# Attention, output projection and feed-forward of an encoder step: three phases against one merged phase

## The chip, the cores and the metric

The kernel runs on one core of one Trainium2 chip. The metric is device time in microseconds (us): the median of three runs before the change is 3194.27 us (3193.53 to 3196.78). The core has five engines with a queue of instructions each: TensorE (PE in the profile, its weight loads PEld), VectorE (DVE), ScalarE (ACT), GpSimd (POOL) and SyncE (SP, which here only issues DMAs). An engine takes its instructions in the order written, and a semaphore makes it wait for another engine.

## The reference

One layer over 2048 prompt rows and 64 sample rows (T = 2112) of width 1024. What the change touches comes after the input projection and the gated linear attention:

```python
def sb_block(q, q_pos, k, v):                       # stick-breaking attention, 4 heads x 64
    z = jnp.einsum('bqhd,bkhd->bhqk', q, k).astype(jnp.float32) * (SB_DH ** -0.5)
    mask = k_pos[None, :] < q_pos[:, None]
    lk = jnp.where(mask, jax.nn.log_sigmoid(-z), 0.0)
    ...                                             # after = sum of lk over the later keys
    A = jnp.exp(jnp.where(mask, jax.nn.log_sigmoid(z) + after, -jnp.inf))
    return jnp.einsum('bhqk,bkhd->bqhd', A.astype(v.dtype), v)
...
out = jnp.concatenate([go, so, co], axis=-1) @ w_out
x = layer_norm(DEEPNORM_ALPHA * x + mix, ln1_g[l], ln1_b[l])
ff = jnp.square(jax.nn.relu(x @ w_up[l])) @ w_down[l]          # 1024 -> 4096 -> 1024
x = layer_norm(DEEPNORM_ALPHA * x + ff, ln2_g[l], ln2_b[l])
```

The exponential of a sum of log-sigmoids is a product of sigmoids, so the kernel computes sigmoid(z) times the running product of sigmoid(-z) over the later keys.

## The kernel before, in words

Five phases run one after the other, with a barrier of all engines between them: `phase_in` (layer norm, x @ w_in), `phase_gla`, `phase_sb` (line 995), `phase_out` (line 1374) and `phase_ffn` (line 1552). The first two are not changed.

**Products in parts.** A float32 operand is split into a high half (rounded to fp32r, by a ScalarE copy) and a low half (operand minus high half, a VectorE subtraction). `split_product` (line 109, its three matmuls are lines 111 to 113) adds high x high, high x low and low x high.

**phase_sb.** Rows are taken in groups of 512 queries; for each head and each block of 512 keys there are four *slots*, one for each 128 queries (168 slots in all, 96 of them over 512 unmasked keys, 64 on the diagonal, 8 of the sample rows). A slot is: scores on TensorE (`ps_z`, three matmuls), two sigmoids on ScalarE (`tg` line 1229, `sg` line 1230), the running product on VectorE (`keep`, the scan of line 1272), and its product with `sg` (`aw`), on VectorE (line 1279) or for every second slot on GpSimd (line 1303). Six slots later `aw` is transposed by TensorE (line 1365, `ps_a`), copied as high half by ScalarE (`ath`, line 1239) and subtracted by VectorE (`atl`, line 1286), and two slots after that multiplied with the values (`ps_o`, three matmuls). Scores and transposes have three PSUM banks each. Queries, keys and values of all rows are kept in SBUF.

**phase_out.** The mixed columns (`mixt_scratch`) times `w_out`, whose halves stay in SBUF; then the residual and layer norm 1 tile by tile (128 rows); its result goes to `x1_scratch` in DRAM.

**phase_ffn.** Groups of 512, 512, 512 and 576 rows. For each group both weight matrices pass through SBUF in units of 128 x 2048 (1 MB): loaded by SP, high half by ScalarE (`wh`, line 1721), low half by VectorE (`wl`, line 1769), in a ring of three. A step `up` makes two blocks of 128 hidden columns (`ps_u`, 24 matmuls for each block and each part of the rows), ScalarE takes relu (line 1738), VectorE squares (line 1783), ScalarE copies the high half (`hh`, line 1743), VectorE subtracts (`hl`, line 1786). A step `down` multiplies eight hidden blocks with `w_down` (`ps_d`) and VectorE adds the result to `res` (line 1761). Between groups TensorE transposes the next rows (line 1842, one bank `ps_t`). Layer norm 2 is VectorE's, with an addition on GpSimd (line 1824).

The order of the work is a list made by Python before any instruction is written (`plan` in `phase_sb`, `order` in the other two); every engine goes through the same list and issues its own part of each entry.

## Time and profile before

| | |
|---|---|
| median of three runs | 3194.27 us |
| span of the profiled execution | 3213.5 us |
| TensorE busy in it | 2880.8 us (90%) |
| VectorE / ScalarE / GpSimd busy | 1621.9 / 1042.7 / 405.2 us |
| mean granted TensorE clock | 0.929 |

The page gives no other time for the profiled execution than its span, which is 19.2 us above the median. Busy is the time in which an engine had an instruction under way; ends of TensorE's matmuls are modelled, and neighbours overlap, so the distance between the starts of two matmuls tells what one costs, and not its duration. The granted clock is a share of full speed: 1.0 is 2.4 GHz, 0.5 is 1.2 GHz. In these times `phase_sb` runs from about 955 us, `phase_out` from about 1395 us and `phase_ffn` from about 1596 us of the span to its end.

### The profile page before, as it was taken

What the parts mean: (1) busy time and instruction counts of PE and PEld (TensorE: products, weight loads), DVE (VectorE), ACT (ScalarE), POOL (GpSimd) and SP (SyncE); (2) the same over time, 40 slices, a digit from 0 to 9 for tenths busy, and PEclk for the clock granted to TensorE, in tenths of its full rate; (3) what the DMA queues carried; (4) which work ended last, traced back from release to release, by engine and by line L of the source; (5) the groups of instructions that cost most, each with busy time, mean ns of one, the idle gap of its engine ahead of it and who ended that gap; (6) DMA issues with size and microseconds to landing.
All of it is one profiled execution on the core that took longest, in us unless ns stands there. A gap on an engine that the chain in (4) does not pass through costs nothing.

```text
span 3213.5 us, 35264 instructions
## 1 busy us (share of the span) xinstructions
PE 2880.8 (90%) x13930; PEld 2308.0 (72%) x13930; DVE 1621.9 (50%) x2127; ACT 1042.7 (32%) x1670; POOL 405.2 (13%) x316
## 2 busy tenths in 40 slices
PE   5999999945559999889879998999989998999998
PEld 4778788834446555567668886888778886889986
DVE  5333331178867999847443343634345433534434
ACT  3333332224435666631032222323222222213321
POOL 1100100076301222203200000200001000100001
PEclk9999999957785899979979998999989998999999
DMA  5445453233322000034243322333223332222221
GB/s 187 162 152 170 162 162 111 85 118 94 78 68 64 23 6 4 11 133 173 85 145 105 118 93 78 118 107 116 92 73 125 122 104 66 79 92 79 79 79 43
DMA packets 206421, 318.23 MB, mean 99 GB/s; under 512 B 17296, under 2 KB 116416, under 8 KB 206256
## 3 DMA queue, kind: packets, MB, share of 16 engines
q1 hardware_dynamic: 177264, 255.26, 25.3%
q0 software_dynamic: 10160, 34.62, 2.9%
q10 hardware_dynamic: 18832, 26.10, 2.2%
q8 instruction: 111, 1.82, 0.2%
q14 instruction: 54, 0.44, 0.0%
HBM read 254.96 MB, written 60.96 MB: 98 GB/s over the span
## 4 chain that ended last, share of the span: by engine, by line
PE 47%; DVE 2%; ACT 1%; issue 0%; DMA 0%; POOL 0%; SPq 0%; ACTq 0%; POOLq 0%
PE p_ps_d L111 8%; PE p_ps_d L112 8%; PE p_ps_d L113 8%; PE p_ps_u L111 7%; PE p_ps_u L112 7%; PE p_ps_u L113 7%; PE p_ps_t L1842 1%; DVE p_xl L1774 1%; ACT p_xh L1728 1%; DVE p_wl L1769 0%; DVE p_res L1814 0%; DVE p_r L1783 0%; ACT p_hh L1743 0%; DVE p_res L1811 0%; ACT p_r L1738 0%
## 5 line engine op out<-in xcount | busy, mean ns | idle before, releaser
L1769 DVE TENSOR_TENSOR p_wl<-p_wst,p_wh 128x2048 fp32r<-128x2048 f32 x128 | 293.3, 2292 | 375.1 <-ACT p_wh L1721 375.1
L111 PE MATMUL p_ps_u<-p_xh,p_wh 128*128 128x512 f32 (+1 forms) x1280 | 453.9, 355 | 14.1 <-DVE p_r L1783 9.2
L113 PE MATMUL p_ps_u<-p_xl,p_wh 128*128 128x512 f32 (+1 forms) x1280 | 453.4, 354 | 0.0
L112 PE MATMUL p_ps_u<-p_xh,p_wl 128*128 128x512 f32 (+1 forms) x1280 | 453.3, 354 | 0.0
L111 PE MATMUL p_ps_d<-p_wh,p_hh 128*128 128x512 f32 (+1 forms) x1088 | 430.3, 395 | 10.4 <-DVE p_hl L1786 10.4
L112 PE MATMUL p_ps_d<-p_wh,p_hl 128*128 128x512 f32 (+1 forms) x1088 | 428.0, 393 | 0.0
L113 PE MATMUL p_ps_d<-p_wl,p_hh 128*128 128x512 f32 (+1 forms) x1088 | 426.9, 392 | 0.0
L1721 ACT ACTIVATE p_wh<-p_wst 128x2048 fp32r<-128x2048 f32 x128 | 244.1, 1908 | 555.7 <-PE p_ps_d L113 549.3
L111 PEld LDWEIGHTS p_ps_u<-p_xh,p_wh 128*128 128x128 f32 x1280 | 243.6, 190 | 45.8 <-DVE p_r L1783 10.1
L113 PEld LDWEIGHTS p_ps_u<-p_xl,p_wh 128*128 128x128 f32 x1280 | 243.5, 190 | 30.2
L112 PEld LDWEIGHTS p_ps_u<-p_xh,p_wl 128*128 128x128 f32 x1280 | 243.5, 190 | 29.9
L1824 POOL TENSOR_TENSOR p_res<-p_res,p_b_b 128x1024 f32<-128x1024 f32 (+1 forms) x17 | 64.1, 3773 | 1527.8 <-DVE p_res L1814 1527.8
L111 PEld LDWEIGHTS p_ps_d<-p_wh,p_hh 128*128 128x128 f32 (+1 forms) x1088 | 203.6, 187 | 59.0 <-DVE p_hl L1786 11.9
L111 PE MATMUL p_ps_m<-p_xh,p_wh 128*128 128x512 f32 (+3 forms) x680 | 242.3, 356 | 1.4 <-DVE p_xl L320 1.4
L112 PE MATMUL p_ps_m<-p_xh,p_wl 128*128 128x512 f32 (+3 forms) x680 | 243.0, 357 | 0.0
L113 PE MATMUL p_ps_m<-p_xl,p_wh 128*128 128x512 f32 (+3 forms) x680 | 241.3, 355 | 0.0
L329 DVE TENSOR_TENSOR p_wl<-p_wst,p_wh 128x512 fp32r<-128x512 f32 (+1 forms) x192 | 127.3, 703 | 223.6 <-ACT p_wh L272 223.5
L113 PEld LDWEIGHTS p_ps_d<-p_wl,p_hh 128*128 128x128 f32 (+1 forms) x1088 | 203.2, 187 | 48.1
L112 PEld LDWEIGHTS p_ps_d<-p_wh,p_hl 128*128 128x128 f32 (+1 forms) x1088 | 203.8, 187 | 46.0
L1783 DVE SCALAR_TENSOR_TENSOR p_r<-p_ps_u,p_r 128x512 f32<-128x512 f32 (+1 forms) x160 | 95.4, 596 | 213.9 <-ACT p_r L1738 213.9
L1761 DVE SCALAR_TENSOR_TENSOR p_res<-p_res,p_ps_d 128x512 f32<-128x512 f32 (+1 forms) x136 | 93.5, 687 | 173.0 <-PE p_ps_d L113 162.2
L1738 ACT ACTIVATE p_r<-p_ps_u 128x512 f32<-128x512 f32 (+1 forms) x160 | 83.4, 521 | 290.9 <-PE p_ps_u L113 290.8
(173 smaller groups left out, 4788.9 us busy)
## 6 DMA issues: line engine op xcount, KB each, us to landing
p_wst<-in_w_up SPq DMA_DIRECT2D x64, 1024.0 KB, 5.4
p_wst<-in_w_down SPq DMA_DIRECT2D x64, 1024.0 KB, 5.0
p_wst<-in_w_in SPq DMA_DIRECT2D x128, 256.0 KB, 3.7
zt_scratch<-p_outb ACTq DMA_DIRECT2D x48, 256.0 KB, 2.0
p_wst<-in_w_in SPq DMA_DIRECT2D x32, 264.0 KB, 3.2
p_xs<-in_x_prompt SPq DMA_DIRECT2D x16, 512.0 KB, 5.5
xn_scratch<-p_xn POOLq DMA_DIRECT2D x16, 512.0 KB, 3.1
p_wst<-in_w_in SPq DMA_DIRECT2D x64, 128.0 KB, 2.6
```

What stands on the lines that cost most here:

```text
L111: pe.matmul(out, lhs_hi, rhs_hi, start=first, stop=False, skip_group_check=skip)
L112: pe.matmul(out, lhs_lo, rhs_hi, start=False, stop=False, skip_group_check=skip)
L113: return pe.matmul(out, lhs_hi, rhs_lo, start=False, stop=last, skip_group_check=skip)
L329: dve.tensor_tensor(wl[:, gc % 2, k, :width], wst[:, u % WSTAGE, :width], wh[:, gc % 2, k, :width].bitcast(F32), ALU.subtract).then_inc(wl ...
L1721: act.activation(wh[:, u % WRING, :], wst[:, u % WSTG, :], ACT.Copy).then_inc(whi_done, 1)
L1728: act.activation(xh[:, 4 * q:4 * q + 4, o:o + c], ps_t[:, :].rearrange("p (k t) -> p k t", k=4)[:, :, :c], ACT.Copy).then_inc(xhi_done, 1)
L1738: act.activation(r[:, i % 2, :cc], ps_u[:, i % 2, :cc], ACT.Relu).then_inc(relu_done, 1)
L1761: dve.scalar_tensor_tensor(out=acc, in0=acc, scalar=ALPHA if c == 0 else 1.0, in1=ps_d[:cc, ti, :], op0=ALU.mult, op1=ALU.add).then_inc(su ...
L1769: dve.tensor_tensor(wl[:, u % WRING, :], wst[:, u % WSTG, :], wh[:, u % WRING, :].bitcast(F32), ALU.subtract).then_inc(wlo_done, 1)
L1774: dve.tensor_tensor(xl[:, 4 * q:4 * q + 4, o:o + c], ps_t[:, :].rearrange("p (k t) -> p k t", k=4)[:, :, :c], xh[:, 4 * q:4 * q + 4, o:o + ...
L1783: dve.scalar_tensor_tensor(out=r[:, i % 2, :cc], in0=ps_u[:, i % 2, :cc], scalar=0.0, in1=r[:, i % 2, :cc], op0=ALU.max, op1=ALU.mult).the ...
L1824: pool.tensor_tensor(res[:c, g % 2, ti, :], res[:c, g % 2, ti, :], b_b[:c, :], ALU.add).then_inc(normed, 1)
```

## The change

`phase_sb`, `phase_out` and `phase_ffn` become one function, `phase_tail` (line 989 of the kernel after), with one list `order`.

- **Two streams.** The stream `dense` holds the output projection and feed-forward of the four groups of rows, the stream `attention` the slots. Group 0's attention and the preparation of all keys and values come first. From there on, `add_attention` puts pieces of the attention stream behind dense steps in proportion to a price of each step (5.4 for `up`, 2.7 for `down` and `out`), such that attention of group g is complete before the output projection of group g. The stretch from the last quarter of an output projection to the transposes behind it has price 0 and gets none, and so does the whole feed-forward of the last group. A `pause` of price 32.4 behind the first output projection puts some attention there without products beside it.
- **Attention in two passes.** Keys are stored in DRAM with their high half in partitions 0 to 63 and the low half in 64 to 127 (`ks_scratch`), the query's halves are present in both; one matmul with 128 rows does both products with the key (lines 1758 and 1759). Values lie as high | low in 128 columns (`vs_scratch`), so each output has two halves of 64 partitions that are added at the end (line 1652). A head takes 256 queries at a time, so the products with the values are twice as many, of up to 256 columns, in two passes (lines 1784 and 1785). Keys, values and queries are loaded anew for each head and block.
- **Banks.** `ps_z`, `ps_a` and `ps_o` have one PSUM bank each, `ps_d` three, `ps_u` two. The transposes between groups use `ps_d`.
- **Weights.** Units of 128 x 1024 (512 KB), 288 in all, ring of four, two stages. The low half is subtracted on GpSimd (line 1669) and not on VectorE. `w_out` passes through the same ring once for each group.
- **Feed-forward.** Chunks of four hidden blocks and not eight, so VectorE adds 272 results of `down` and 68 of `out` (136 and 34 before). ScalarE makes the high half as the square of relu (line 1479); VectorE squares the SBUF copy (line 1592).
- **Layer norm.** Two VectorE instructions of 1024 columns (lines 1556 and 1559) take the place of two on VectorE and one on GpSimd; the root of the variance is a power on GpSimd, 128 x 1 (line 1665), and not a square root on ScalarE. Layer norm 1 stays in SBUF (`x1_scratch` is gone).

```diff
-def phase_sb(nc, a, zt_dram, mixt_dram, k_p, v_p, k_s, v_s):
-    ZB, AB = 3, 3
-    SIG, AW, AT = 4, 3, 3
-    TURN_LAG, WEIGH_LAG = 6, 8
...
-def phase_out(nc, mixt_dram, w_out, ln_g, ln_b, xn_dram, x1_dram):
-    RAW, STAGE, BANKS = 4, 4, 6
...
-def phase_ffn(nc, x1_dram, w_up, w_down, ln_g, ln_b, ident_in, y_tile, lasting):
-    NF = 8
-    WRING, WSTG = 3, 2
+def phase_tail(nc, a, zt_dram, mixt_dram, xn_dram, ks_dram, vs_dram, k_p, v_p, k_s, v_s, y_tile, lasting):
+    NF = 4
+    WRING, WSTG, DB = 4, 2, 3
+    SIG, KEEP, AW = 2, 3, 3
...
+        ps_u, ps_d = s.ps("ps_u", [P, 2, 512]), s.ps("ps_d", [P, DB, 512])
+        ps_z, ps_a, ps_o = s.ps("ps_z", [P, 512]), s.ps("ps_a", [P, 512]), s.ps("ps_o", [P, 512])
...
+        for g in range(SEQ // 512):
+            for b in range(2):
+                for h in range(SBH):
+                    diag = (g, 512, [(0, P), (P, P)], [P * (2 * b + 1), P * (2 * b + 2)], [(P * x, P, max(0, x - 2 * b)) for x in range(2 * b + 2)])
+                    full = [(c, 512, [(0, P), (P, P)], [512, 512], [(P * x, P, 0) for x in range(4)]) for c in range(g - 1, -1, -1)]
+                    add_head(h, 512 * g + 256 * b, 256, [diag] + full)
...
+        due, at = [], 0.0
+        for u, _, _ in items:
+            at = max(units[u]["slot1"] + 1, at + 0.5)
+            due.append(int(at))
...
+        cost = {"up": 5.4, "down": 2.7, "out": 2.7, "pause": 2.7}
+        price = [0.0 if i in quiet or i >= mixed[-1] else cost.get(st[0], 0.0) * (st[1] if st[0] == "pause" else 1) for i, st in enumerate(dense)]
...
+        def add_attention(upto):
+            nonlocal put
+            order.extend(attention[put:upto])
+            put = max(put, upto)
...
+        def split_weights(i):
+            nonlocal next_w
+            while next_w < len(wunits) and (next_w < WRING or unit_end[next_w - WRING] < i):
+                order.append(("w", next_w))
+                if next_w + WSTG < len(wunits):
+                    order.append(("w_load", next_w + WSTG))
+                next_w += 1
...
+        begun, spent = put, 0.0
+        for i, st in enumerate(dense):
+            if i in mixed:
+                add_attention(group_end[st[1]])
+            if st[0] in ("up", "down", "out"):
+                order.append(st)
+                split_weights(i)
+            elif st[0] == "mix":
+                order.append(st)
+                if st[2] + 4 < KT:
+                    order.append(("mix_load", st[1], st[2] + 4))
+            elif st[0] != "pause":
+                order.append(st)
+            spent += price[i]
+            if i < mixed[-1]:
+                add_attention(begun + int((len(attention) - begun) * spent / sum(price)))
+        assert put == len(attention) and next_w == len(wunits)
...
-                            act.activation(hh[:, slot_of(c, f), o:o + cc], r[:, i % 2, :cc], ACT.Copy).then_inc(sq_done, 1)
+                        act.activation(hh[:, hidden_at(c, f), o:o + cc], r[:, i % 2, :cc], ACT.Square).then_inc(hh_done, 1)
...
-                    dve.tensor_tensor(wl[:, u % WRING, :], wst[:, u % WSTG, :], wh[:, u % WRING, :].bitcast(F32), ALU.subtract).then_inc(wlo_done, 1)
-                            dve.scalar_tensor_tensor(out=r[:, i % 2, :cc], in0=ps_u[:, i % 2, :cc], scalar=0.0, in1=r[:, i % 2, :cc],
+                        dve.tensor_tensor(r[:, i % 2, :cc], r[:, i % 2, :cc], r[:, i % 2, :cc], ALU.mult).then_inc(sq_done, 1)
...
-                    dve.tensor_scalar(acc, acc, mv[:c, sl, 0:1], rstd[:c, sl, :], ALU.subtract, ALU.mult).then_inc(centred, 1)
-                    dve.tensor_tensor(acc, acc, g_b[:c, :], ALU.mult).then_inc(scaled, 1)
-                    pool.tensor_tensor(res[:c, g % 2, ti, :], res[:c, g % 2, ti, :], b_b[:c, :], ALU.add).then_inc(normed, 1)
+                dve.scalar_tensor_tensor(out=acc, in0=acc, scalar=mv[:c, 0:1], in1=g_b[:c, :], op0=ALU.subtract, op1=ALU.mult).then_inc(scaled, 1)
+                dve.scalar_tensor_tensor(out=acc, in0=acc, scalar=rstd[:c, :], in1=b_b[:c, :], op0=ALU.mult, op1=ALU.add).then_inc(ln_done, 1)
...
+                    pool.tensor_tensor(rstd[:c, :], veps[:c, :], power[:c, :], ALU.pow).then_inc(rstd_done, 1)
+                if what == "w":
+                    u = at[0]
+                    pool.wait_ge(whi_done, u + 1)
+                    pool.tensor_tensor(wl[:, u % WRING, :], wst[:, u % WSTG, :], wh[:, u % WRING, :].bitcast(F32), ALU.subtract).then_inc(wlo_done, 1)
...
-                        mm = split_product(pe, out, qh[pb:pb + 64, pr, q], ql[pb:pb + 64, pr, q], kh[pb:pb + 64, pr, ks_], kl[pb:pb + 64, pr, ks_],
+                        pe.wait_ge(sig_done, 2 * n)
+                    pe.matmul(ps_z[:m, :w], qh[:, sl, o:o + m], kk[:, u % 2, :w], start=not un["diag"], stop=False, skip_group_check=True)
+                    pe.matmul(ps_z[:m, :w], ql[:, sl, o:o + m], kk[:, u % 2, :w], start=False, stop=True, skip_group_check=True).then_inc(z_done, 1)
...
-            mm = split_product(pe, ps_o[:, u["o"] % 2, c0:c1], vh[:kn, vt, hc], vl[:kn, vt, hc], ath[:kn, ai % AT, c0:c1], atl[:kn, ai % AT, c0:c1],
+                    for x, (k0, kn, i0, off, nq) in enumerate(turned_columns(k)[0]):
+                        out, vs = ps_o[:, P * i0:P * i0 + nq], vv[:kn, u % 2, y + x, :]
+                        pe.matmul(out, vs, ath[:kn, k % 2, off:off + nq], start=opens and x == 0, stop=False, skip_group_check=True)
+                        mm = pe.matmul(out, vs, atl[:kn, k % 2, off:off + nq], start=False, stop=k + 1 == heads[j]["item1"], skip_group_check=True)
+                    mm.then_inc(av_done, 1)
...
-        phase_sb(nc, a, zt_dram, mixt_dram, k_p, v_p, k_s, v_s)
-        phase_out(nc, mixt_dram, a["w_out"][0], a["ln1_g"][0], a["ln1_b"][0], xn_dram, x1_dram)
-        phase_ffn(nc, x1_dram, a["w_up"][0], a["w_down"][0], a["ln2_g"][0], a["ln2_b"][0], a["ident"], y_tile, lasting)
+        phase_tail(nc, a, zt_dram, mixt_dram, xn_dram, ks_dram, vs_dram, k_p, v_p, k_s, v_s, y_tile, lasting)```

**ScalarE's queue in the feed-forward.** `p_r` is relu, `p_hh` the high half of the hidden block, `p_wh` that of a weight unit. Before, in the first group:

```order
L1721 ACTIVATE p_wh<-p_wst 128x2048 x5
L1738 ACTIVATE p_r<-p_ps_u 128x512
L1743 ACTIVATE p_hh<-p_r 128x512
L1738 ACTIVATE p_r<-p_ps_u 128x512
L1743 ACTIVATE p_hh<-p_r 128x512
L1721 ACTIVATE p_wh<-p_wst 128x2048
```

Now, in the first group as well (`p_tg`, `p_sg` are the sigmoids of a slot, `p_ath` the high half of transposed weights of attention, `p_otmp` a head's output):

```order
L1472 ACTIVATE p_r<-p_ps_u 128x512
L1479 ACTIVATE p_hh<-p_r 128x512
L1449 ACTIVATE p_wh<-p_wst 128x1024
L1524 ACTIVATE p_otmp<-p_ps_o 64x256
L1509 ACTIVATE p_tg<-p_ps_z 128x512
L1510 ACTIVATE p_sg<-p_ps_z 128x512
L1517 ACTIVATE p_ath<-p_ps_a 128x384
L1449 ACTIVATE p_wh<-p_wst 128x1024
```

The sigmoids and the copy for attention stand behind relu, square and weight copy of the dense step that they follow.

**VectorE's queue in the feed-forward.** `p_wl` is the low half of a weight unit, `p_hl` that of the hidden block, `p_res` the sum. Before:

```order
L1783 SCALAR_TENSOR_TENSOR p_r<-p_ps_u,p_r 128x512
L1786 TENSOR_TENSOR p_hl<-p_r,p_hh 128x512
L1769 TENSOR_TENSOR p_wl<-p_wst,p_wh 128x2048 x2
L1761 SCALAR_TENSOR_TENSOR p_res<-p_res,p_ps_d 128x512 x4
L1769 TENSOR_TENSOR p_wl<-p_wst,p_wh 128x2048 x2
```

Now (`p_keep` is the scan, `p_aw` its product with `sg`, `p_atl` the low half of the transposed weights, `p_ql` that of a query):

```order
L1640 TENSOR_TENSOR p_aw<-p_sg,p_keep 128x512
L1540 SCALAR_TENSOR_TENSOR p_res<-p_res,p_ps_d 128x512
L1630 SCALAR_TENSOR_TENSOR p_keep<-p_tg,p_keep,p_zero 128x513
L1540 SCALAR_TENSOR_TENSOR p_res<-p_res,p_ps_d 128x512
L1645 TENSOR_TENSOR p_atl<-p_ps_a,p_ath 128x512
L1615 TENSOR_TENSOR p_ql<-p_qraw,p_qh 128x256
L1540 SCALAR_TENSOR_TENSOR p_res<-p_res,p_ps_d 128x512
L1645 TENSOR_TENSOR p_atl<-p_ps_a,p_ath 128x512
L1540 SCALAR_TENSOR_TENSOR p_res<-p_res,p_ps_d 128x512 x2
```

The weight halves are gone from this queue, and single additions alternate with pieces of a slot.

**GpSimd's queue.** Before, at the end of attention and the start of the output projection:

```order
L1303 TENSOR_TENSOR p_aw<-p_sg,p_keep 128x256
L1303 TENSOR_TENSOR p_aw<-p_sg,p_keep 128x512 x7
L1303 TENSOR_TENSOR p_aw<-p_sg,p_keep 64x512 x4
L74 UNCONDITIONAL_BRANCH
L76 ISA
L1507 UNCONDITIONAL_BRANCH
L1515 TENSOR_TENSOR p_y<-p_y,p_b_b 128x1024
```

Now, across the change from one group of rows to the next:

```order
L1669 TENSOR_TENSOR p_wl<-p_wst,p_wh 128x1024 x4
L1678 TENSOR_TENSOR p_aw<-p_sg,p_keep 128x512
L1669 TENSOR_TENSOR p_wl<-p_wst,p_wh 128x1024 x2
L1665 TENSOR_TENSOR p_rstd<-p_veps,p_power 128x1 x3
L1669 TENSOR_TENSOR p_wl<-p_wst,p_wh 128x1024 x2
L1665 TENSOR_TENSOR p_rstd<-p_veps,p_power 128x1
L1669 TENSOR_TENSOR p_wl<-p_wst,p_wh 128x1024 x5
```

GpSimd has the weight halves, every second slot's product and the power of each layer norm in one queue.

## Rows read from the trace of the kernel before

**Rows 1.** Stages: busy us (count) of PE, PEld, DVE, ACT, POOL; clock; DMA share; GB/s
```profile
955.00:1395.00 440.00, 391.40 (x1718) 241.00 (x1718) 373.44 (x497) 262.27 (x601) 91.82 (x84) 0.82 0.09 24
1399.00:1596.00 197.00, 190.28 (x816) 153.88 (x816) 117.41 (x172) 31.14 (x55) 48.31 (x32) 0.97 0.42 148
1596.00:1634.70 38.70, 8.82 (x32) 5.73 (x32) 10.20 (x15) 8.67 (x11) 2.88 (x2) 0.53 0.35 117
1634.70:1966.40 331.70, 328.86 (x1441) 271.96 (x1442) 132.70 (x122) 95.10 (x94) 0.00 (x0) 0.99 0.34 111
1966.40:1984.10 17.70, 7.54 (x34) 5.15 (x32) 5.95 (x9) 4.18 (x7) 0.00 (x0) 0.61 0.00 0
3198.00:3213.50 15.50, 2.51 (x11) 1.21 (x9) 6.26 (x9) 0.29 (x1) 5.79 (x4) 0.64 0.25 85
```

**Rows 2.** PE in time order in the feed-forward: start, duration, line, tiles
```profile
1700.13 0.39 PE L111 MATMUL p_ps_d<-p_wh,p_hh 128*128 128x512 f32 x1
...
1705.80 0.39 PE L112 MATMUL p_ps_d<-p_wh,p_hl 128*128 128x512 f32 x1
...
2899.76 0.29 PE L113 MATMUL p_ps_u<-p_xl,p_wh 128*128 128x288 f32 x1
...
2904.67 0.29 PE L111 MATMUL p_ps_u<-p_xh,p_wh 128*128 128x288 f32 x1
```

**Rows 3.** PE in time order: one slot of the attention stage
```profile
1248.34 0.49 PE L111 MATMUL p_ps_z<-p_kh,p_qh 64*128 64x512 f32 x1
...
1249.23 0.66 PE L1365 MATMUL p_ps_a<-p_ident,p_aw 128*128 128x128 f32 x4
1249.64 0.47 PE L111 MATMUL p_ps_o<-p_ath,p_vh 128*64 128x512 f32 x1
...
1250.49 0.49 PE L111 MATMUL p_ps_z<-p_kh,p_qh 64*128 64x512 f32 x1
```

**Rows 4.** Groups of the attention stage: busy, mean ns of one | idle before
```profile
L1272 DVE TENSOR_TENSOR_SCAN p_keep<-p_tg,p_keep,p_zero 128x512 f32<-128x512 f32 x96 | 149.6, 1558 | 11.6 <-ACT p_tg L1229 11.6
L1286 DVE TENSOR_TENSOR p_atl<-p_ps_a,p_ath 128x512 fp32r<-128x512 f32 x112 | 75.7, 678 | 3.8 <-ACT p_ath L1239 3.8
L1239 ACT ACTIVATE p_ath<-p_ps_a 128x512 fp32r<-128x512 f32 x112 | 67.6, 603 | 10.5 <-PE p_ps_a L1365 10.0
L1230 ACT ACTIVATE p_sg<-p_ps_z 128x512 f32<-128x512 f32 x112 | 66.4, 593 | 0.0
```

**Rows 5.** Groups of the output projection and the feed-forward
```profile
L1452 ACT ACTIVATE p_wh<-p_wst 128x1024 fp32r<-128x1024 f32 x8 | 8.5, 1060 | 10.6 <-DMA p_wst<-in_w_out 10.6
L1505 DVE TENSOR_TENSOR p_y<-p_y,p_g_b 128x1024 f32<-128x1024 f32 x16 | 19.6, 1227 | 0.5
L1515 POOL TENSOR_TENSOR p_y<-p_y,p_b_b 128x1024 f32<-128x1024 f32 x16 | 39.3, 2457 | 153.7 <-DVE p_y L1505 153.7
L1743 ACT ACTIVATE p_hh<-p_r 128x512 fp32r<-128x512 f32 x96 | 60.8, 633 | 96.0 <-DVE p_r L1783 96.0
L1761 DVE SCALAR_TENSOR_TENSOR p_res<-p_res,p_ps_d 128x512 f32<-128x512 f32 x128 | 88.1, 688 | 171.7 <-PE p_ps_d L113 161.7 <-DVE p_res L1761 0.5
L1802 DVE BATCH_NORM_STATS2 p_stats<-p_res 128x6 f32<-128x512 f32 x16 | 11.0, 689 | 0.1
```

**Rows 6.** VectorE and GpSimd side by side in layer norm 2
```profile
2025.29 2.29 DVE L1769 TENSOR_TENSOR p_wl<-p_wst,p_wh 128x2048 fp32r<-128x2048 f32 x1
2025.52 4.33 POOL L1824 TENSOR_TENSOR p_res<-p_res,p_b_b 128x1024 f32<-128x1024 f32 x1 [423.56 <-DVE p_res L1814]
...
2028.87 1.53 DVE L1786 TENSOR_TENSOR p_hl<-p_r,p_hh 128x512 fp32r<-128x512 f32 x1 [0.70 <-ACT p_hh L1743]
...
2031.70 0.69 DVE L1786 TENSOR_TENSOR p_hl<-p_r,p_hh 128x512 fp32r<-128x512 f32 x1 [0.70 <-ACT p_hh L1743]
```

**Rows 7.** DMA issues of the page: KB each, us to landing
```profile
p_wst<-in_w_up SPq DMA_DIRECT2D x64, 1024.0 KB, 5.4
```

**Rows 8.** Small GpSimd operation of the convolution, by form
```profile
L959 POOL COPY p_cu<-p_cu 128x2 f32<-128x2 f32 x6 | 4.5, 742 | 21.1 <-DMA p_cb<-zt_scratch 21.1
```

1420 lines of the change are left out of this document (659 added, 761 removed).

## The prediction, made before the changed kernel ran

> **What bounds the kernel now.** I read the stages first [rows 1]: from 955 us to the end, 2258.5 us, the work is in the three phases that the change merges. In the steady feed-forward TensorE is the bound: 328.9 us of 331.7 busy at a granted clock of 0.99, with VectorE at 132.7 us. The time order there [rows 2] shows an even beat: 25 matmuls of 512 columns from 1700.13 to 1705.80, so 0.227 us each, and 37 of 288 columns from 2899.76 to 2904.67, so 0.133 us each. The attention stage is different: 440 us in which VectorE is busy for 373 and TensorE for 391. One of its slots [rows 3] takes 2.15 us: scores 0.89, four transposes 0.41, products with values 0.85. VectorE needs almost the same for a slot [rows 4]: scan 1.56, subtraction 0.68, half a product of 0.69 (the size of rows 6), 2.6 us with the waits in it. So there neither leaves much to the other, but the stage also starts badly: mean clock 0.82, where the feed-forward has 0.99. Between the stages TensorE nearly stands: 38.7 us with 8.8 busy before the feed-forward, 17.7 with 7.5 at a change of group, each at a clock of 0.53 to 0.61.
>
> **Dense products.** The change leaves their number alone: 2304 matmuls of 512 columns for `up` in groups 0 to 2, 1536 of 288 in group 3, 3264 for `down`, 816 for the output projection. 6384 x 0.2268 = 1448 us, 1536 x 0.1327 = 204, and 34 times four transposes at 0.41 [rows 3] = 14. Sum 1666 us.
>
> **TensorE's part of attention.** One score matmul of three goes (0.89 - 0.23 = 0.66 us), the transposes stay (0.41), and instead of three products of 512 columns a slot has four of up to 256. No row has 256 columns; below stands 0.113 us (half of 0.227), above 0.133 (the row with 288). I take 0.13, so 0.53 plus 0.09 for the switch. A full slot is 1.69 us, for 2.15. 96 x 1.69 = 162; 64 diagonal slots with shorter operands at 1.3, my estimate from the same parts, = 83; 8 sample slots and 42 transposes of keys 12. Sum 257 us, of which some 25 (19 slots) lie in the opening, before any dense product, and 232 among or between dense steps. The gain is that VectorE's 2.6 us per slot now stand beside dense products, and the stretches at low clock go: TensorE is what the time is made of.
>
> **The opening.** It prepares all keys and values, six blocks, one staging buffer each, and runs 19 slots. A block: twice (transposes 0.41, two copies at 0.60, two subtractions at 0.68) = 5.9 us, a copy of 1.06 and a subtraction of 1.23 [rows 5] for the values, then stores that must land before the next block writes, about 3: 11 us. Three slots of group 0 between, at some 3 us each, since with one bank for scores the next slot waits for both sigmoids. 6 x 20 = 120 us. Bounds: 75 if the slots fit into the waits of the blocks, 150 if they don't and each DMA costs the 5.4 us of the largest one [rows 7].
>
> **The first group and the borders.** The first products wait for mixed rows, 8 us. Behind the first output projection the pause has four slots and two layer norms that nothing covers, then eight groups of transposes: 24 us beyond the slots counted above. At each of three group changes the output projection must wait until relu, square and low half of the last `up` and four split inputs are through: 0.6 + 0.6 + 4 x 0.87 and a few waits, 6 us; and the first `up` waits for the last transposes, 5 us; with some us at the lower clock behind each, as after the stops in rows 1, 15 us for a change that now costs 17.7. 45 us. Layer norm 1 stands between four `out` steps of 2.7 us: two statistics of 0.69, two instructions of 1.23 [rows 5] and the power on GpSimd, for which VectorE waits. The power has no row: it is at most the 0.74 us of a small copy [rows 8], at least nothing, but a weight half of 2.46 us can stand before it. 5 to 6 us for each of four tiles against 13.6 us of products and two spare banks leaves about 4 us, over four groups 15. The end (last addition, layer norm, store) is 15.5 us now and 14 without GpSimd's addition.
>
> **Weight halves on GpSimd.** 288 units at 2.46 us [rows 5] are 708 us of a queue with almost nothing else, beside some 2000 us. A unit's way behind an `up`: relu 0.6, square 0.63, high half 1.06, low half 2.46: 4.75 us, and the ring lets it be needed only after another step of 24 x 0.227 = 5.44 us. The load is half the bytes of the 5.4 us DMA [rows 7], and with two stages a stage has two steps for load, high and low half: 5.4 + 1.06 + 2.46 = 8.9 against 10.9. So I cost this at nothing, covered by dense products. If the cover goes (low half at 4.33, [rows 6]) the two figures are 10.85 against 10.9: just even. VectorE loses 128 x 2.29 = 293 us of halves [rows 6] and gains 170 additions x 0.69 = 117 [rows 5]; it was no bound in the feed-forward and needs about 60% of the time there with attention.
>
> **New waits.** The list gives every engine one order, with one bank each for scores and for transposes. The second block of transposes of a unit waits for VectorE's low half of the first, behind the scan, behind the sigmoids, which stand in ScalarE's queue behind relu, square and weight copy of the step in front. From the end of an `up`: 0.6 + 0.63 + 1.06 + 0.6 = 2.9 us to the first sigmoid's end, at which GpSimd has just begun a low half; scan 1.56 (a mean with some waits in it; up to 2.4 more behind a low half), low half 0.68, and some tenths for signals: between 5.5 and 8 us. Cover: scores 0.66, transposes 0.41 and one `up`, 6.5; with a `down` in its place 3.8. In the new list the two blocks of transposes follow each other with no dense step between only 8 times in 156, transposes and their products with values 5 times. So a wait per slot lies between 0 and, where a `down` is the only cover, 2 to 3 us; most pairs have an `up` or two `down`s. I take 0.4 us for each of 149 slots: 60 us.
>
> **Sum.** 955 (unchanged) + 120 + 8 + 24 + 1666 + 232 + 45 + 15 + 14 = 3079 us without new waits, 3139 with them. The profiled execution before has a span of 3213.5 us, the median is 3194.3, so a factor of 0.994: **3120 us**, 74 us (2.3%) less.
>
> **GpSimd and VectorE on one pair of ports.** A low half of 2.29 us on VectorE and an addition begun 0.23 us later on GpSimd took 4.33 us, and VectorE's next subtraction of two SBUF operands took 1.53 us where one alone took 0.69 [rows 6]: they ran one after the other. With attention, for each group, GpSimd's 72 x 2.46 = 177 us and VectorE's scans, squares, subtractions, products and norms of two SBUF operands (50 x 1.56 + 64 x 0.69 + 25 x 0.69 + 16 x 1.23 = 159 us) take turns: 336 of some 460 us. That fits, with queueing that the 0.4 us above hold. The Trainium skill (SBUF — State Buffer, section "SBUF: two separate sides") says that the pair is locked for a whole instruction and the loser is blocked fully; by that rule the case is the third rival below, the trace agrees with the rule, and it does not show which engine wins when both queue up.
>
> **Rivals.**
> 1. *The waits are covered fully* and the opening overlaps well (75 us). For it: the 13 adjacent pairs are few. Against: in the attention stage of now one signal chain already limits. 3079 - 45 = 3034, x 0.994 = 3016 us.
> 2. *The chain through one bank is the bound* (slower). Every unit waits at TensorE for a low half, as if covered by a `down` alone. At 1.6 us for each of 149 slots 238 us, 3317 in the profile, 3297 us. It decides from 0.9 us per slot on (3213.5 - 3079 = 134.5 over 149). For it: lag of two slots instead of six, one bank instead of three. Against: dense steps between nearly all pairs.
> 3. *The shared ports make weight halves late.* Low halves at 4.33 us, the stage loop at its limit, 1 us more for each of 96 `up` units beside attention: 3139 + 96 = 3235, 3216 us.
> 4. *The change does not hide anything*: TensorE's work in attention was 391 of 440 us. Had it all to be paid again, 955 + 120 + 1666 + 391 + 106 = 3238, 3218 us. Against it: the busy time overlaps and is at a low clock; the starts of rows 3 give 257.
>
> **How the numbers follow.** Forecast (3065 to 3180 us) 0.62; rival 1 0.15; rival 2 0.12; rivals 3 and 4 together 0.08; 0.03 within 0.2% of 3194 us, which is about what a measurement of this kernel can tell from no change. Faster: 0.62 + 0.15 and 0.01 of the third's lower side = 0.78; same 0.03; slower 0.19. The range reaches into rival 1 and over rivals 3 and 4: 3015 to 3225 us. It leaves out rival 2 and part of rival 1.
>
> **What would show it.** Right: TensorE beats of 0.227 us with attention in between at a clock near 1; the low-half line of GpSimd at 2.3 to 2.6 us mean, and few waits of TensorE for it; a first dense product at about 1083 us; an end of group 0's feed-forward some 450 us after its first `up`. Wrong: transposes of attention waiting for the low half line 1645 by more than 60 us in sum, and the clock at 0.5 in short pieces through the groups (rival 2); a mean of 4 us on line 1669 and waits of the first matmul of an `up` for it (rival 3); TensorE's starts in a slot no closer than 2.15 us (rival 4); an opening of over 150 us.

## The result: 4.6% slower, not 2.3% faster

| | before | after |
|---|---|---|
| median (lowest to highest), us | 3193.90 (3193.49 to 3196.78) | 3342.76 (3335.89 to 3348.53) |
| span of the profiled execution, us | 3213.5 | 3334.1 |
| mean granted TensorE clock | 0.929 | 0.917 |

The ratio is 1.0459, with a 95% interval of 1.0442 to 1.0475. The forecast of 3120 us and its range of 3015 to 3225 are both missed, on the far side of no change.

The page of the changed kernel: busy time and share of each engine, three groups of instructions (busy us, mean ns | idle time of the engine before them and what ended it), the granted clock in 40 slices, and one DMA.

```profile
PE 2791.5 (84%) x13838; PEld 2299.2 (69%) x13838; DVE 1672.1 (50%) x2175; ACT 1077.0 (32%) x1783; POOL 1072.1 (32%) x571
...
PEclk9999999868865889999998999989899998999998
...
L1669 POOL TENSOR_TENSOR p_wl<-p_wst,p_wh 128x1024 fp32r<-128x1024 f32 x288 | 742.9, 2594 | 1098.5 <-ACT p_wh L1449 1098.5
L1540 DVE SCALAR_TENSOR_TENSOR p_res<-p_res,p_ps_d 128x512 f32<-128x512 f32 (+1 forms) x340 | 231.9, 684 | 491.0 <-PE p_ps_d L113 470.3
...
L1771 PE MATMUL p_ps_a<-p_ident,p_aw 128*128 128x128 f32 (+2 forms) x564 | 101.7, 305 | 173.8 <-DVE p_atl L1645 143.0
...
p_wst<-in_w_up SPq DMA_DIRECT2D x128, 512.0 KB, 4.1
```

TensorE is busy for 89 us less than before, in a span 121 us longer. No engine is full. The line to stop at is the third group: TensorE stood for 173.8 us ahead of the transposes of attention. The same stages as in [rows 1], in the merged phase: opening, groups with attention, and the last stretch, which has none after 2790 us.

```profile
955.00:1107.00 152.00, 45.32 (x186) 35.54 (x186) 60.68 (x92) 52.01 (x108) 17.50 (x13) 0.52 0.64 203
1107.00:2790.00 1683.00, 1459.69 (x6635) 1187.62 (x6636) 916.60 (x1015) 576.97 (x949) 668.61 (x306) 0.93 0.33 106
2790.00:3334.00 544.00, 507.75 (x2863) 438.61 (x2861) 235.61 (x334) 133.47 (x215) 198.83 (x87) 0.97 0.25 80
```

The middle row holds the loss: in its 1683 us TensorE is busy for 1460, at a clock of 0.93 where the feed-forward alone had 0.99. What TensorE waited for from 955 us on (us in total, times, longest):

```profile
PE p_ps_a L1771 <- DVE p_atl L1645: 143.0, 41, 9.8
PE p_ps_a L1745 <- DMA p_res<-out_new_sb_k_p: 29.2, 3, 14.1
PE p_ps_a L1771 <- POOL p_aw L1678: 23.2, 3, 14.9
PE p_ps_d L111 <- issue: 22.5, 4, 10.2
PE p_ps_d L111 <- DVE p_res L1540: 20.3, 8, 5.0
PE p_ps_d L111 <- DVE p_xl L1566: 18.4, 1, 18.4
PE p_ps_z L1757 <- DMA p_kk<-ks_scratch: 14.2, 1, 14.2
```

One wait leads all others: the one bank of the turned weights, released by VectorE's subtraction `p_atl`. GpSimd's weight halves (`p_wl`, line 1669) are in no row of this view. To see why the release comes late, one such wait in time order (start, duration, engine, line, tiles [idle before, releaser]); the first row is the block of transposes that fills the bank:

```profile
1293.79 0.60 PE L1771 MATMUL p_ps_a<-p_ident,p_aw 128*128 128x128 f32 x4
...
1295.88 2.69 POOL L1669 TENSOR_TENSOR p_wl<-p_wst,p_wh 128x1024 fp32r<-128x1024 f32 x1 [4.22 <-ACT p_wh L1449]
...
1296.22 3.42 DVE L1630 TENSOR_TENSOR_SCAN p_keep<-p_tg,p_keep,p_zero 128x513 f32<-128x513 f32 x1
...
1297.21 0.60 ACT L1517 ACTIVATE p_ath<-p_ps_a 128x512 fp32r<-128x512 f32 x1
...
1300.62 1.27 DVE L1630 TENSOR_TENSOR_SCAN p_keep<-p_tg,p_keep,p_zero 128x513 f32<-128x513 f32 x1
...
1302.24 2.43 POOL L1669 TENSOR_TENSOR p_wl<-p_wst,p_wh 128x1024 fp32r<-128x1024 f32 x1 [3.68 <-ACT p_wh L1449]
1302.51 2.72 DVE L1594 TENSOR_TENSOR p_hl<-p_r,p_hh 128x512 fp32r<-128x512 f32 x1
...
1305.14 0.68 DVE L1645 TENSOR_TENSOR p_atl<-p_ps_a,p_ath 128x512 fp32r<-128x512 f32 x1
...
1305.97 0.88 PE L1771 MATMUL p_ps_a<-p_ident,p_aw 128*128 128x128 f32 x3 [6.11 <-DVE p_atl L1645]
...
1307.49 0.63 PE L113 MATMUL p_ps_d<-p_wl,p_hh 128*128 128x512 f32 x1
...
1307.92 0.63 PE L111 MATMUL p_ps_d<-p_wh,p_hh 128*128 128x512 f32 x1
```

`p_ath` was ready at 1297.81, but `p_atl` began at 1305.14: in VectorE's queue there stood ahead of it two scans, a product, an addition, and square and low half of the next `up`. Two of these ended only a little after a weight half that GpSimd had begun before them: a scan of 3.42 us, where the next took 1.27, ended 1.07 us after the half, and a `p_hl` of 2.72 us, where one alone takes 0.69, ended 0.56 us after it. From the transposes to the release it is 12.0 us, 4.2 of them from these two delays, and TensorE, with one `up` in between, stood for 6.1 of them. Behind the stop matmuls of 512 columns are 0.43 us apart, not 0.227. The granted clock of the same place:

```profile
1303.00:1309.80 6.80, 3.83 (x11) 3.19 (x12) 4.01 (x4) 1.44 (x2) 4.58 (x3) 0.50 0.27 77
1309.80:1367.80 58.00, 53.48 (x257) 43.25 (x255) 29.46 (x31) 21.62 (x35) 21.83 (x10) 1.00 0.33 106
```

TensorE had begun no matmul after 1299.47; the clock fell to 1.2 GHz at 1303.0 and came back to 2.4 GHz at 1309.8, 3.8 us after the work had. Between 1107 and 2790 us there are 38 such pieces at 1.2 GHz, 232 us together.

**Where the time went, summed from the starts of matmuls.** A distance of more than 0.75 us between two starts is counted as a stop (less 0.3 us, the matmul's own); all others are beats, at either clock. From 1107 us to the end: beats at full clock 1780.4, at half clock 166.9 (so 83.5 lost by the clock), stops 239.5, of which 160.7 stand ahead of the transposes of line 1771 (38 stops). Up to 2790 us there are 60 stops, and 37 of the 38 pieces at 1.2 GHz overlap the end of a stop or begin just behind it. The forecast in the profile was 3139 us and the span is 3334, 195 more: opening and first mixed rows 152 for 128, +24; TensorE's own work 1883 for 1898 (beats without the clock's loss 1863.8, and 0.3 for each of 66 stops), -15; stops at transposes 160.7 for 60, +101; clock +83; all other stops 79 for 84, -5 (the 84 held some us of low clock as well); the rest, the end above all, about +7. In medians the miss is 223 us: these 195, 19 for the forecast's factor of 0.994, and 9 by which the median of the changed kernel lies above its profiled span.

### The profile page after: what moved, and what is told of

Its sections match the earlier page's. It is cut to its first block and busy times, and to the rows that moved or that the text cites. A ratio compares the mean times of both kernels' runs of the same rounds, so it can differ in the third digit from the quotient of the medians.

```text
span 3334.1 us, 37193 instructions
## 1 busy us (share of the span) xinstructions
PE 2791.5 (84%) x13838; PEld 2299.2 (69%) x13838; DVE 1672.1 (50%) x2175; ACT 1077.0 (32%) x1783; POOL 1072.1 (32%) x571
## 5 line engine op out<-in xcount | busy, mean ns | idle before, releaser
L1669 POOL TENSOR_TENSOR p_wl<-p_wst,p_wh 128x1024 fp32r<-128x1024 f32 x288 | 742.9, 2594 | 1098.5 <-ACT p_wh L1449 1098.5
L1540 DVE SCALAR_TENSOR_TENSOR p_res<-p_res,p_ps_d 128x512 f32<-128x512 f32 (+1 forms) x340 | 231.9, 684 | 491.0 <-PE p_ps_d L113 470.3
L111 PE MATMUL p_ps_u<-p_xh,p_wh 128*128 128x512 f32 (+1 forms) x1280 | 469.3, 367 | 6.9 <-DVE p_xl L1585 5.3
L111 PE MATMUL p_ps_d<-p_wh,p_hh 128*128 128x512 f32 (+1 forms) x1088 | 444.7, 409 | 22.3 <-DVE p_res L1540 20.3
L112 PE MATMUL p_ps_u<-p_xh,p_wl 128*128 128x512 f32 (+1 forms) x1280 | 461.8, 361 | 0.0
L113 PE MATMUL p_ps_u<-p_xl,p_wh 128*128 128x512 f32 (+1 forms) x1280 | 461.0, 360 | 0.0
L112 PE MATMUL p_ps_d<-p_wh,p_hl 128*128 128x512 f32 (+1 forms) x1088 | 434.0, 399 | 0.0
L113 PE MATMUL p_ps_d<-p_wl,p_hh 128*128 128x512 f32 (+1 forms) x1088 | 432.8, 398 | 0.0
L1449 ACT ACTIVATE p_wh<-p_wst 128x1024 fp32r<-128x1024 f32 x288 | 294.2, 1051 | 251.1 <-PE p_ps_d L113 216.0
L1592 DVE TENSOR_TENSOR p_r<-p_r 128x512 f32<-128x512 f32 (+1 forms) x160 | 111.5, 697 | 485.2 <-ACT p_hh L1479 484.7
L1472 ACT ACTIVATE p_r<-p_ps_u 128x512 f32<-128x512 f32 (+1 forms) x160 | 83.7, 523 | 620.8 <-PE p_ps_u L113 606.3
L111 PEld LDWEIGHTS p_ps_u<-p_xh,p_wh 128*128 128x128 f32 x1280 | 249.0, 195 | 39.4 <-DVE p_xl L1585 6.2
L113 PEld LDWEIGHTS p_ps_u<-p_xl,p_wh 128*128 128x128 f32 x1280 | 247.2, 193 | 34.2
L112 PEld LDWEIGHTS p_ps_u<-p_xh,p_wl 128*128 128x128 f32 x1280 | 248.5, 194 | 30.6
L111 PEld LDWEIGHTS p_ps_d<-p_wh,p_hh 128*128 128x128 f32 (+1 forms) x1088 | 207.2, 190 | 72.0 <-DVE p_res L1540 24.8
L1771 PE MATMUL p_ps_a<-p_ident,p_aw 128*128 128x128 f32 (+2 forms) x564 | 101.7, 305 | 173.8 <-DVE p_atl L1645 143.0
L111 PE MATMUL p_ps_m<-p_xh,p_wh 128*128 128x512 f32 (+3 forms) x680 | 242.2, 356 | 1.4 <-DVE p_xl L320 1.4
L112 PE MATMUL p_ps_m<-p_xh,p_wl 128*128 128x512 f32 (+3 forms) x680 | 242.7, 357 | 0.0
L113 PEld LDWEIGHTS p_ps_d<-p_wl,p_hh 128*128 128x128 f32 (+1 forms) x1088 | 206.7, 190 | 50.7
L113 PE MATMUL p_ps_m<-p_xl,p_wh 128*128 128x512 f32 (+3 forms) x680 | 241.1, 355 | 0.0
L112 PEld LDWEIGHTS p_ps_d<-p_wh,p_hl 128*128 128x128 f32 (+1 forms) x1088 | 207.3, 191 | 43.8
## 6 DMA issues: line engine op xcount, KB each, us to landing
p_wst<-in_w_up SPq DMA_DIRECT2D x128, 512.0 KB, 4.1
p_wst<-in_w_down SPq DMA_DIRECT2D x128, 512.0 KB, 3.5
p_wst<-in_w_out SPq DMA_DIRECT2D x32, 512.0 KB, 3.5
```

What stands on the lines that cost most here:

```text
L111: pe.matmul(out, lhs_hi, rhs_hi, start=first, stop=False, skip_group_check=skip)
L112: pe.matmul(out, lhs_lo, rhs_hi, start=False, stop=False, skip_group_check=skip)
L113: return pe.matmul(out, lhs_hi, rhs_lo, start=False, stop=last, skip_group_check=skip)
L1449: act.activation(wh[:, u % WRING, :], wst[:, u % WSTG, :], ACT.Copy).then_inc(whi_done, 1)
L1472: act.activation(r[:, i % 2, :cc], ps_u[:, i % 2, :cc], ACT.Relu).then_inc(relu_done, 1)
L1540: dve.scalar_tensor_tensor(out=acc, in0=acc, scalar=scale, in1=ps_d[:c, d % DB, :], op0=ALU.mult, op1=ALU.add).then_inc(d_free, 1)
```

## The experiments

All times are medians; ratios are to the kernel before in runs on the same chip, with their 95% intervals. The edits are to the changed kernel, where nothing else is said. "Stops" and "half clock" are the sums just described, from 1107 us to the end. A gain or loss in us is a difference between two medians that were taken at different times. The kernel before ran from 3189.27 to 3225.58 us beside the experiments, and its medians went from 3193.90 to 3205.08, so a difference of some 10 us says little by itself.

**x1, GpSimd's subtraction nearly empty** (this part of the low halves isn't computed).

```diff
-                    pool.tensor_tensor(wl[:, u % WRING, :], wst[:, u % WSTG, :], wh[:, u % WRING, :].bitcast(F32), ALU.subtract).then_inc(wlo_done, 1)
+                    n = 1024 if u < WRING else 8
+                    pool.tensor_tensor(wl[:, u % WRING, :n], wst[:, u % WSTG, :n], wh[:, u % WRING, :n].bitcast(F32), ALU.subtract).then_inc(wlo_done, 1)
```

> GpSimd's subtraction of a weight unit's low half is cut from 1024 to 8 columns for all units but the first four; that part of the computation is left out, every wait stays. Theory A (the waits at the transposes come from GpSimd holding the ports that VectorE needs: a scan of 3.42 us where one alone takes 1.27): the wait of line 1771 for line 1645, 143 us in sum, falls below 40 us, the clock in the groups with attention rises to 0.97 or more, and the time falls by 150 us or more, from 3343 to below 3190 us. Theory B (the waits come from one PSUM bank and the place of the subtraction in VectorE's queue, whatever GpSimd does): the wait stays above 100 us and the time above 3280 us.

Measured: 3236.12 us, 1.0093 [1.0060, 1.0127], 107 us less than the changed kernel, between the two theories (under 3190, over 3280 us). Full-width scans, `p_hl` and `p_atl` in the changed kernel (first fence) and in x1 (second), busy us and mean ns:

```profile
L1630 DVE TENSOR_TENSOR_SCAN p_keep<-p_tg,p_keep,p_zero 128x513 f32<-128x513 f32 x95 | 200.7, 2113 | 5.7 <-ACT p_tg L1509 5.5
L1594 DVE TENSOR_TENSOR p_hl<-p_r,p_hh 128x512 fp32r<-128x512 f32 x96 | 74.6, 777 | 3.3
L1645 DVE TENSOR_TENSOR p_atl<-p_ps_a,p_ath 128x512 fp32r<-128x512 f32 x108 | 73.2, 677 | 26.4 <-ACT p_ath L1517 26.3
```

```profile
L1630 DVE TENSOR_TENSOR_SCAN p_keep<-p_tg,p_keep,p_zero 128x513 f32<-128x513 f32 x95 | 121.7, 1281 | 7.1 <-ACT p_tg L1509 7.0
L1645 DVE TENSOR_TENSOR p_atl<-p_ps_a,p_ath 128x512 fp32r<-128x512 f32 x108 | 73.4, 679 | 25.4 <-ACT p_ath L1517 25.2
...
L1594 DVE TENSOR_TENSOR p_hl<-p_r,p_hh 128x512 fp32r<-128x512 f32 x96 | 66.4, 692 | 3.3
```

What follows: GpSimd's work made VectorE's scans 0.83 us longer each, and left `p_atl`, which reads PSUM, as it was. VectorE's whole busy time falls from 1672.1 to 1420.3 us though it has the same 2175 instructions; after the scans its products `p_aw` gain most (84 of them, 116.7 us down to 49.6). TensorE's waits at the transposes in x1:

```profile
PE p_ps_a L1772 <- DVE p_atl L1645: 73.9, 26, 5.8
...
PE p_ps_a L1772 <- POOL p_aw L1679: 29.9, 5, 14.9
```

The first halves, from 143.0 to 73.9 us, and doesn't go: the ports are a large part of the loss, and something else is behind the rest. The second, for GpSimd's own products, doesn't fall (23.2 before), and no wait of TensorE for a weight half is on record in either run, so nothing here puts the gain down to GpSimd's shorter queue.

**x2, the same subtractions on VectorE,** in the place of its queue where the list has them.

```diff
+                if what == "w":
+                    u = at[0]
+                    dve.wait_ge(whi_done, u + 1)
+                    dve.tensor_tensor(wl[:, u % WRING, :], wst[:, u % WSTG, :], wh[:, u % WRING, :].bitcast(F32), ALU.subtract).then_inc(wlo_done, 1)
-                if what == "w":
-                    u = at[0]
-                    pool.wait_ge(whi_done, u + 1)
-                    pool.tensor_tensor(wl[:, u % WRING, :], wst[:, u % WSTG, :], wh[:, u % WRING, :].bitcast(F32), ALU.subtract).then_inc(wlo_done, 1)
```

> The low halves go back to VectorE at the same places of the list, the rest stays. Theory A: a half takes 1.23 us of VectorE instead of 2.6 us of the shared ports, scans fall back to below 1.4 us mean, and the time falls by 60 to 130 us. Theory B: 288 halves of 1.23 us stand in VectorE's queue in front of the subtractions that the transposes wait for, the wait grows from 143 us, and the time rises by 20 us or more.

Measured: 3322.07 us, 1.0361 [1.0323, 1.0399], 21 us less than the changed kernel by the medians and 31 by the ratios, so neither theory's size (60 to 130 us less, 20 or more longer).

```profile
L1565 DVE TENSOR_TENSOR p_wl<-p_wst,p_wh 128x1024 fp32r<-128x1024 f32 x288 | 345.4, 1222 | 11.5 <-ACT p_wh L1449 11.4
L1634 DVE TENSOR_TENSOR_SCAN p_keep<-p_tg,p_keep,p_zero 128x513 f32<-128x513 f32 x96 | 122.8, 1280 | 3.3 <-ACT p_tg L1509 3.3
```

Scans are back at 1280 ns, and VectorE has 288 subtractions of 1222 ns more, 345 us. Its busy time is 1735.6 us, 64 more than with the halves on GpSimd. What follows: moving 743 us of work to GpSimd relieved VectorE of those 64 us only, and the wait for `p_atl` falls only from 143.0 to 125.2 us.

**x3, two banks for `ps_d` and not three** (`WRING, WSTG, DB = 4, 2, 2`), the control for x4.

> Control for the next kernel: the dense stream has two PSUM banks instead of three, everything else stays. Both theories: dense products wait for VectorE's additions more often, 30 to 120 us slower than 3343 us.

Measured: 3385.00 us, 1.0554 [1.0515, 1.0593]; TensorE waits 38.8 us for `p_res` (20.3 with three banks) and 141.0 for `p_atl`. The bank is worth 42 us by the medians, 30 by the ratios.

**x4, that bank given to the turned weights.** Every other use of `ps_a` gets the number of its bank as an index; those lines are left out here.

```diff
-    WRING, WSTG, DB = 4, 2, 3
+    WRING, WSTG, DB = 4, 2, 2
-        ps_z, ps_a, ps_o = s.ps("ps_z", [P, 512]), s.ps("ps_a", [P, 512]), s.ps("ps_o", [P, 512])
+        ps_z, ps_a, ps_o = s.ps("ps_z", [P, 512]), s.ps("ps_a", [P, 2, 512]), s.ps("ps_o", [P, 512])
...
-                    if x:
-                        pe.wait_ge(a_free, x)
+                    if x >= 2:
+                        pe.wait_ge(a_free, x - 1)
```

> As the control, with the third bank of the dense stream given to the transposes of attention, which so have two. Theory B: the second transposes of a unit no longer wait for the first one's low half; the wait falls below 30 us and the time is 120 us or more below the control's. Theory A: VectorE is late in any case, the wait moves to the products with the values (line 1784) and to the dense banks, and the time is within 50 us of the control's.

Measured: 3232.32 us, 1.0086 [1.0056, 1.0117]. TensorE's waits in x4:

```profile
PE p_ps_d L111 <- DVE p_res L1540: 51.4, 26, 7.7
PE p_ps_o L1784 <- DVE p_atl L1645: 46.3, 16, 13.7
PE p_ps_a L1745 <- DMA p_res<-out_new_sb_k_p: 30.9, 3, 14.5
PE p_ps_z L1757 <- DVE p_ql L1615: 26.4, 15, 3.0
```

The wait at the transposes is gone, and 110 us of time with it, 153 against its control x3. That the bank's release was the leading wait is shown, and the gain is theory B's. Three other replies of VectorE now take its place, two of them where theory A had them: the late engine is the same, and it is asked elsewhere.

**x5, the subtraction ahead of the scan** in the list.

```diff
-            attention += [("turn", k) for k in turns[:1]] + [("weigh", k) for k in weighs]
+            attention += [("turn", k) for k in turns[:1]] + [("lo", k) for k in turns[:1]] + [("weigh", k) for k in weighs]
...
-            attention += [("lo", k) for k in turns[:1]]
```

> Only the list of the attention stream changes: a block's low half (VectorE) stands directly behind its transposes and no longer behind the scan of the slot. Theory C (the chain is long because the scan, 2.1 us on the mean, stands in VectorE's queue in front of the subtraction that frees the one bank): the wait of line 1771 falls from 143 us to 50 to 90 us, the time to 3240 to 3290 us. Rival D (the chain is long because ScalarE comes late, behind relu, square and weight copy, so the scan in front costs nothing): wait and time as before within 20 us, as the scan now starts later instead.

Measured: 3248.56 us, 1.0144 [1.0100, 1.0189]; 94 us less, with no more hardware and no less work. The wait at transposes is down from 143.0 us (the forecast was 50 to 90):

```profile
PE p_ps_a L1770 <- DVE p_atl L1644: 91.9, 28, 14.7
```

So more than a third of it was only the place of one instruction in VectorE's queue. That what is left is the chain itself, where two blocks of transposes are close, is tested by x12.

**x6, the transposes further apart.** The list's due times (the attention slot at which each block of transposes is placed) put up to two blocks of transposes on one attention slot; here nearly all get a slot each.

```diff
-        for u, _, _ in items:
-            at = max(units[u]["slot1"] + 1, at + 0.5)
+        for u, y, _ in items:
+            at = max(units[u]["slot1"] + 1, at + (0.5 if y and units[u]["head"] >= 32 else 1.0))
```

> The due times of a unit's two blocks of transposes lie one slot apart instead of half a slot (the last blocks of the sample rows excepted), so both no longer stand in one slot. Pairs with 0 or 2.7 us of dense products between them fall from 22 to 8, those with 5.4 us rise from 45 to 60. Theory C/B (cover between two blocks is too short): 30 to 80 us faster than 3343. If what counts is only VectorE's lateness and not the place: within 20 us.

Measured: 3283.02 us, 1.0256 [1.0211, 1.0302]; 60 us less, 119.2 us of waits at transposes in 33 stops.

**x7, no two streams:** all of attention ahead of the first feed-forward step (`add_attention(len(attention))`, one line added ahead of the loop over dense steps).

> All attention is put before the first dense step, with the same banks, the same list otherwise. The interleaving is what the change is for: without it all 168 slots pay their own chain, some 2.9 to 4 us each instead of 1.7 us of TensorE beside dense work. If interleaving still gains in the kernel after: 3430 to 3600 us. If the waits eat all of it: 3343 us or less.

Measured: 3411.41 us, 1.0660 [1.0603, 1.0716], clock 0.901. So putting attention between dense products does gain, 69 us, less than the 87 or more of the forecast (3430 to 3600 us). But the attention that it puts there is slower by itself than that of before: the first dense product starts at 1593.1 us, 486 us later than in the changed kernel, for the 149 slots moved ahead of it, 3.3 us each, where before 168 slots and the keys took 440 us, 2.6 each. It has more and shorter stops at the same place (68 of at most 2.8 us), and its full-width scans take 1317 ns on average, so these stops are not the ports':

```profile
PE p_ps_a L1772 <- DVE p_atl L1646: 132.7, 68, 2.8
```

```profile
L1631 DVE TENSOR_TENSOR_SCAN p_keep<-p_tg,p_keep,p_zero 128x513 f32<-128x513 f32 x96 | 126.4, 1317 | 19.0 <-ACT p_tg L1510 18.8
```

**x8, the kernel before with two of the three products** in scores and values, and nothing else of the change (the key's low half and that of attention's weights are left out). One of the three places is shown; the scores on the diagonal and the products with the values are edited alike.

```diff
+def two(pe, out, lhs_hi, lhs_lo, rhs_hi, first, last):
+    pe.matmul(out, lhs_hi, rhs_hi, start=first, stop=False, skip_group_check=True)
+    return pe.matmul(out, lhs_lo, rhs_hi, start=False, stop=last, skip_group_check=True)
...
-                        mm = split_product(pe, out, qh[pb:pb + 64, pr, q], ql[pb:pb + 64, pr, q], kh[pb:pb + 64, pr, ks_], kl[pb:pb + 64, pr, ks_],
-                                            False, True, skip=True)
+                        mm = two(pe, out, qh[pb:pb + 64, pr, q], ql[pb:pb + 64, pr, q], kh[pb:pb + 64, pr, ks_], False, True)
```

> The kernel before, with two matmuls instead of three in the scores and in the products with the values of attention; the part that is left out is the key's low half and the low half of the weights of attention. TensorE saves 0.45 us of 2.15 per slot. If VectorE's queue is the bound of that stage: within 15 us of 3194. If TensorE is: 60 us less or more.

Measured: 3213.56 us, 1.0025 [0.9997, 1.0053]: no gain, and 19 us above 3194, a little outside the 15 of the forecast. Its attention stage, in the same window, to be held against the first row of [rows 1]:

```profile
955.00:1395.00 440.00, 405.35 (x1363) 234.85 (x1363) 366.97 (x494) 266.25 (x599) 91.66 (x84) 0.61 0.09 23
```

Of 1718 matmuls 355 are gone, VectorE works as long as before (367 for 373 us), and the granted clock is 0.61 for 0.82. The stage is no shorter: its last product with values starts at 1396.2 us, and before at 1389.0. Here the stage gave TensorE's saving back as a lower clock, and the two passes by themselves brought nothing.

**x9 to x12, combinations.** x9 is x4 with x5; x10 is x9 with x6; x11 is x10 with x2; x12 is x5 with x6, its banks as in the changed kernel. The edits are those shown.

> The changed kernel with three edits: VectorE's subtraction for the turned weights ahead of the scan (as in x5), two PSUM banks for the turned weights, and for these two instead of three banks for the dense products (as in x4). Theory of the wait chain through one bank: x4 gained 110 us and x5 94 us, each for the same 160.7 us of stops ahead of the transposes, so they cannot add up. With two banks the transposes wait no more; the first product with a turned tile (46.3 us behind p_atl in x4) is what the earlier subtraction still helps. I expect 3232 - 46 x 0.8 = 3195, between 3175 and 3215, and the wait behind p_atl under 20 us. Rival (the dense products' waits for a free bank, 51.4 us in x4, are now the bound): within 10 us of x4, 3222 to 3242.

Measured: 3216.44 us, 1.0033 [1.0008, 1.0059]. The wait at transposes is gone, 49.5 us for `p_res` and 35.1 for `p_atl` ahead of the products with values are left. The gain over x4 is 16 us in medians, just outside the ranges of both theories, and the wait behind `p_atl` is not under 20 us. The first wait is now that for a free dense bank, which x4 gave away.

> x9 and the due times a whole step apart for nearly all attention slots (as in x6). If stops ahead of transposes are gone by x9 already, moving the slots apart has only the wait for p_ql and for the next dense bank left to shorten: 5 to 20 us faster than x9, 3175 to 3200. Rival (the later slots reach into the end, where fewer dense products are left to fill): 10 to 30 us slower than x9.

Measured: 3231.44 us, 1.0079 [1.0051, 1.0106], 15 us slower than x9, as the rival has it, though its reason wasn't tested. The waits for `p_res` grew to 55.7 us and those for `p_ql` from 24.6 to 37.9.

> x10 with the low halves of the weights on VectorE. Theory of the shared ports: GpSimd's 288 x 2.6 us lengthen VectorE's scans from 1.28 to 2.12 us, and where x2 gained 21 us over the changed kernel, most was that VectorE's reply came earlier. With the bank chain open the reply is less urgent, so the gain shrinks to 0 to 15 us: 3165 to 3200. Rival (VectorE, which takes 345 us of subtractions on, is the bound now): 10 to 40 us slower than x10.

Measured: 3184.73 us, 0.9941 [0.9914, 0.9968]: 47 us less than x10. I had expected a gain of 0 to 15; that the time lies in my 3165 to 3200 is luck, as x10 was slower than I had thought. Neither theory holds, the rival not even in sign: the move is worth more with the one-bank chain open (47 us for 21). That doesn't say that GpSimd's lock costs more then; x14 below tells the two parts apart. The wait for `p_res`, in the same queue of VectorE, goes from 55.7 us to 34.4, that for `p_ob` ahead of the products with values from 28.2 to 19.9.

> The changed kernel with the subtraction ahead of the scan and the due times apart, its banks as they were (one for the turned weights, three for the dense products). x5 gained 94 and x6 60 us of 143 to 161 us of stops; 91.9 us were left in x5 in 28 stops, which are slots close behind each other. Expected: the stops go to 30 us or less, 3249 - 0.7 x 62 = 3205, between 3185 and 3225. Rival (what is left in x5 is not from slots that follow closely): 3240 to 3255.

Measured: 3191.45 us, 0.9956 [0.9935, 0.9978]. The two edits of the list alone take back 151 us, nearly the sum of x5 and x6 (94 and 60). At the transposes 35.1 us are left, for 30 or less in the forecast, in 7 stops:

```profile
PE p_ps_a L1770 <- DVE p_atl L1644: 35.1, 7, 13.7
```

Three dense banks and one for the turned weights, in the right order, beat two and two (x10) by 40 us.

**x13 and x14: what the halves cost once the order is right.** x13 is x12 with x2, x14 is x12 with x1.

> x12 with the low halves of the weights as 288 subtractions on VectorE instead of GpSimd. If the lock on the shared ports still costs PE when the reply is ahead of the scan: x11 against x10 shows 47 us for this same edit with two transpose banks, of which I expect two thirds here, x12 - 30 = 3160, between 3145 and 3180, ratio to before 0.985 to 0.992. Rival (with three dense banks VectorE's own 350 us of subtractions are what is late): within 10 us of x12, 3182 to 3200.

Measured: 3157.53 us, 0.9856 [0.9819, 0.9893], with 3160 forecast: **the fastest version that does all the work,** 1.4% under the kernel before and 5.8% under the changed one (0.9856 over 1.0459). x11 and x12 are under the kernel before as well, by 0.6 and 0.4%. Its waits, and its stages:

```profile
PE p_ps_a L1744 <- DMA p_res<-out_new_sb_k_p: 31.2, 3, 14.4
PE p_ps_a L1770 <- DVE p_atl L1648: 24.0, 7, 13.7
PE p_ps_z L1756 <- DVE p_ql L1618: 23.6, 13, 4.3
PE p_ps_d L111 <- DVE p_res L1539: 21.2, 10, 4.4
```

```profile
1107.00:2790.00 1683.00, 1575.21 (x7503) 1293.56 (x7504) 1040.81 (x1382) 613.35 (x1012) 127.63 (x103) 0.97 0.36 115
2790.00:3157.00 367.00, 345.32 (x1991) 301.86 (x1989) 170.54 (x248) 89.94 (x148) 7.59 (x5) 0.97 0.25 77
```

In the same 1683 us it gets through 7503 matmuls where the changed kernel had 6635, at a clock of 0.97 for 0.93, and with VectorE at 1040.8 us for 916.6: more of VectorE's time, less of its lateness.

> x12 with GpSimd's subtraction cut to 8 of its 1024 columns after the first four units (this part of the low halves isn't computed). In the changed kernel the same cut gave 107 us. With the one-bank chain open by order and due times, most of that was the chain's: I expect 40 to 60 us here, 3130 to 3150. Rival (the two costs are separate and add up): 3191 - 107 = 3085, between 3070 and 3100.

Measured: 3117.32 us, 0.9730 [0.9694, 0.9767]: 74 us under x12, more than the 40 to 60 expected and less than the rival's 107. Of these 74, x13 gets 34 with the work done in full; the other 40 are the price of 288 subtractions in VectorE's queue. With the order as it was, the same two differences are 107 us for the halves on GpSimd (x1) and 86 for those on VectorE (x1 against x2). So with the order mended GpSimd's halves cost less than before, 74 for 107, and VectorE's fell further, 40 for 86: that is why the move pays more.

**All of it in one table.** If stops of TensorE and the clock behind them are the whole story, the change of the two sums must give the change of the span. In the rows of the table it does within 7 us:

| | stops | half clock costs | change of both | change of span |
|---|---|---|---|---|
| after | 239.5 | 83.5 | | 3334.1 |
| x1 no low halves | 150.3 | 65.6 | -107 | -103 |
| x2 halves on VectorE | 220.7 | 85.9 | -16 | -12 |
| x4 two banks | 158.4 | 54.8 | -110 | -104 |
| x5 low half first | 167.4 | 70.5 | -85 | -87 |
| x6 apart | 201.2 | 74.2 | -48 | -53 |
| x12 = x5 + x6 | 136.9 | 44.4 | -142 | -144 |
| x13 = x12 + x2 | 108.3 | 39.4 | -175 | -177 |
| x14 = x12 + x1 | 76.0 | 32.8 | -214 | -219 |

Of the runs not in it, x7, x9, x10 and x11 agree as well (+66 for +72, -122 for -117, -100 for -102, -147 for -151), and x3 is off by 10 (+40 for +50). From the changed kernel to x13, 131 us of stops went and 44 us of what half clock costs, a third of a us for each. In the other rows it is 0.18 to 0.38, and in x2 half clock cost 2 us more with 19 us of stops less.

## Why the prediction was wrong

**Right: what TensorE has to do.** Beats of 0.227 us and two passes give 1883 us of matmuls for a forecast of 1898. Rival 4, nothing hidden, falls by that. Weight halves of 2594 ns on average are in the 2.3 to 2.6 us of the forecast, and TensorE never waits for one; rival 3 as written falls too. Rival 1, waits covered fully, falls by the stops at transposes. The other stops (changes of group, first group, layer norm 1) are 79 us for 84.

**The step that failed: "New waits", 0.4 us for each of 149 slots.** They were 160.7 us, 1.08 us a slot, and what decided was put at 0.9. That is rival 2, to which I gave 0.12; its time of 3297 us, at 1.6 us a slot, was still under the 3342.76 measured, for the clock is on top. At the 1.08 us measured its own working gives 3220 us, so part of its nearness is a wait that it had too large. Three things were wrong in the working.
- I counted one slot's own chain (sigmoid, scan, subtraction: 5.5 to 8 us), and not VectorE's queue. In the stretch shown two scans, a product, an addition and the next `up`'s square and low half stood ahead of `p_atl`: 12.0 us, 4.2 of them by GpSimd's halves. x5 shows it: the same instructions in another order, 94 us.
- I set the cover at 6.5 us from the list and counted the 8 places with none, and took a mean for the rest. A mean hides the close pairs: setting them apart alone gave 60 us (x6), and with the order mended as well 7 stops were left of 41 (x12).
- The low clock was kept for the changes of group. But 38 pieces at 1.2 GHz lay in the middle of dense work, 37 of them at a stop, and the low clock cost 83 us in all.

**The cost put at nothing: weight halves on GpSimd.** I asked whether the halves would be late for TensorE, and whether both engines' time on the ports fits (336 of 460 us). Both answers were right and beside the point: the ports' price is paid by VectorE, whose replies TensorE waits for. It made VectorE's busy time 252 us longer (1672.1 for 1420.3 in x1) and cost 107 us of the kernel's time, 74 with the order mended. On VectorE the same halves cost 86 and 40, so what the choice of GpSimd lost is 21 and 34 us, and no placing of them was free. Rows 6 of before held it: a subtraction of 1.53 us for 0.69. I took it for the total of two engines and not for a delay in the chain of the paragraph above it. The Trainium skill (SBUF — State Buffer, section "SBUF: two separate sides") says that whichever of the two starts first has the pair for its whole instruction; the stretch shown agrees, with a scan begun 0.34 us behind a weight half and ended 1.07 us after it, within 0.2 us of the 1.27 that a scan alone takes. One sum of the forecast's ring has a slip (5.4 + 1.06 + 4.33 is 10.79 and not 10.85), which changes nothing.

**The opening** took 152 us for 120 + 8. The largest single waits in it are for the staged rows of the next block (29.2 us in 3) and for the mixed rows (18.4 where I had 8). Its first part, without the mixed rows, is 134 us, within the bounds of 75 to 150 and above the 120 chosen. The 3 us for the stores of a block had no row behind them: the stores to `ks_scratch` and `vs_scratch` take 4.3 and 4.8 us from issue to landing.

**Layer norm 1.** The power, bounded by 0.74 us from a small copy, takes 1.52 us. The row gives the shortest, median and longest in ns:

```profile
L1665 POOL TENSOR_TENSOR p_rstd<-p_veps,p_power x34: 1520/1521/1549, 1155.7 to 3327.1; 128x1 f32<-128x1 f32 x32, 64x1 f32<-64x1 f32 x2
```

VectorE waited 15.1 us for it over 34 tiles. The bound was no bound, but with 34 of them it is small.

**The factor of 0.994.** I took the profiled execution of before, 19.2 us above the median, for a share that holds for any kernel. It was one of that kernel's longer executions: they went from 3189.27 to 3225.58 us. The profiled execution of the changed kernel, with a span of 3334.1 us, is the run of 3335.89 us. The factor took 19 us off the forecast without a reason.

**What stays open.** Whether two dense banks and slots apart (x10) lose to x9 by reason of the list's end or of the dense banks was not told apart. The opening was not tested by a run of its own; it is some 24 us of the loss, and in all runs with two streams the first dense product starts within 8 us of where it does in the changed kernel.

## What to carry to other kernels

When a buffer is released by another engine, price the wait by everything that stands ahead of the release in that engine's queue, between the two uses, and not by the releasing chain; then look for the pairs with the least cover, not the mean. Before giving more banks, try the release earlier in the list: here two edits of the list were worth 151 us, where a second bank, taken from the dense products, was worth 110. Work with two SBUF operands moved from VectorE to GpSimd was here not off VectorE (64 us relieved for 743 moved): price it as a delay of each VectorE instruction with two SBUF operands that TensorE waits for.

## What was not expected of the hardware

- VectorE paid most of the shared ports' price. GpSimd's subtractions, shortest, median and longest in ns:

```profile
L1669 POOL TENSOR_TENSOR p_wl<-p_wst,p_wh x288: 2335/2418/3353, 991.1 to 3290.0; 128x1024 fp32r<-128x1024 f32 x144
```

  Their mean of 2594 is 176 ns above the median, 51 us over 288 of them (75 us above the shortest); VectorE lost 252 us. Its scans go from 1269 ns at the shortest to 3505 at the longest.
- With 355 of 1718 matmuls less in the attention stage, the granted clock fell from 0.82 to 0.61 (x8), and TensorE's busy time even rose, from 391 to 405 us.
- A stop of 6.1 us was followed by another 3.8 us at 1.2 GHz, and the clock fell during the stop and not at its end.
- The power of 128 x 1 on GpSimd takes 1.52 us, twice a copy of 128 x 2 [rows 8].
